# Eight seven-product units instead of seven per pair of column blocks in the first down projection, and an earlier last batch of activation sums

## The reference, cut to what matters

```python
def swiglu(x, w_gate, w_up, w_down):
    return (jax.nn.silu(x @ w_gate) * (x @ w_up)) @ w_down

h = h + 0.5 * swiglu(rms_norm(h, ffn1_norm), ffn1_w_gate, ffn1_w_up, ffn1_w_down)
...
h = h + 0.5 * swiglu(rms_norm(h, ffn2_norm), ffn2_w_gate, ffn2_w_up, ffn2_w_down)
```

## Time and profile before

| | us |
|---|---|
| median of 3 runs | 1835.87 (1835.83 to 1838.89) |
| the profiled execution | 1837.03 |
| its span, first to last instruction | 1834.9 |
| TensorE busy in the span | 1817.6 (99%) |
| VectorE busy | 1504.9 (82%) |
| ScalarE busy | 997.4 (54%) |
| mean clock granted to TensorE | 0.999 of full |

### The profile page before, as it was taken

One profiled execution on the slowest core, in us unless ns is written; L12 is line 12 of the kernel. 1 busy time (PEld: TensorE's weight loads), 2 busy tenths in 40 slices (PEclk: granted clock), 3 DMA queues, 4 the chain that ended last, 5 costly groups with the idle time before them and its releaser, 6 DMA issues.

```text
span 1834.9 us, 29704 instructions
## 1 busy us (share of the span) xinstructions
PE 1817.6 (99%) x10674; PEld 1544.7 (84%) x10674; DVE 1504.9 (82%) x1754; ACT 997.4 (54%) x1181; POOL 11.1 (1%) x23
## 2 busy tenths in 40 slices
PE   8999999999999999999999999999999999999998
PEld 7888888888888888999998878888888888888886
DVE  5888888888998986688966866688888888899996
ACT  7455555555555655754535665545555555555554
POOL 1000000000000000000000000000000000000000
PEclk9999999999999999999999999999999999999999
DMA  7767776777766778565433558577767677676664
GB/s 239 230 212 222 231 221 206 227 218 233 241 199 210 220 227 266 176 185 143 139 111 108 175 171 264 178 229 234 230 220 233 216 226 225 218 237 199 208 216 149
DMA packets 207850, 380.35 MB, mean 207 GB/s; under 512 B 16016, under 2 KB 35728, under 8 KB 207504
## 3 DMA queue, kind: packets, MB, share of 16 engines
q1 hardware_dynamic: 206768, 377.08, 65.3%
q10 hardware_dynamic: 480, 1.97, 0.3%
q0 software_dynamic: 512, 0.06, 0.0%
HBM read 360.19 MB, written 18.87 MB: 207 GB/s over the span
## 4 chain that ended last, share of the span: by engine, by line
PE 92%; DVE 3%; DMA 2%; ACT 1%; issue 1%; SPq 0%; ACTq 0%; DVEq 0%
PE psA L427 30%; PE psB L427 28%; PE psB L1231 6%; PE psT L438 5%; PE psM L438 5%; PE psA L438 5%; PE psA L1231 4%; PE psB L438 2%; PE psM L427 1%; DVE wlo L410 1%; DMA raw<-in_w_in 1%; PE psA L1242 1%; PE psB L650 1%; DMA raw<-in_ffn_w_down 0%; DVE y L1455 0%
## 5 line engine op out<-in xcount | busy, mean ns | idle before, releaser
L401 ACT CAST whi<-raw 128x1024 fp32r<-128x1024 f32 (+1 forms) x648 | 676.6, 1049 | 693.6 <-DVE raw L1455 186.1
L410 DVE TENSOR_TENSOR wlo<-raw,whi 128x1024 fp32r<-128x1024 f32 (+1 forms) x648 | 771.8, 1214 | 205.2 <-ACT whi L401 192.4
L427 PE MATMUL psA<-whi,xh 128*128 128x512 f32 (+1 forms) x576 | 221.8, 385 | 0.5 <-DVE wlo L410 0.5
L427 PE MATMUL psA<-whi,xl 128*128 128x512 f32 (+1 forms) x576 | 221.2, 384 | 0.0
L427 PE MATMUL psA<-wlo,xh 128*128 128x512 f32 (+1 forms) x576 | 221.2, 384 | 0.0
L427 PE MATMUL psB<-whi,xh 128*128 128x512 f32 x544 | 211.7, 389 | 0.0
L427 PE MATMUL psB<-whi,xl 128*128 128x512 f32 x544 | 211.6, 389 | 0.0
L427 PE MATMUL psB<-wlo,xh 128*128 128x512 f32 x544 | 211.6, 389 | 0.0
L427 PEld LDWEIGHTS psA<-whi,xh 128*128 128x128 f32 x576 | 108.4, 188 | 22.0 <-DVE wlo L410 0.7
L427 PEld LDWEIGHTS psA<-whi,xl 128*128 128x128 f32 x576 | 108.4, 188 | 21.3
L427 PEld LDWEIGHTS psA<-wlo,xh 128*128 128x128 f32 x576 | 108.4, 188 | 21.1
(11 more groups left out here) (511 smaller groups left out, 3436.7 us busy)
## 6 DMA issues: line engine op xcount, KB each, us to landing
raw<-in_ffn_w_gate SPq DMA_DIRECT2D x176, 512.0 KB, 4.5
raw<-in_ffn_w_up SPq DMA_DIRECT2D x176, 512.0 KB, 4.6
raw<-in_ffn_w_down SPq DMA_DIRECT2D x176, 512.0 KB, 4.5
raw<-in_w_in SPq DMA_DIRECT2D x80, 512.0 KB, 3.7
raw<-in_w_out SPq DMA_DIRECT2D x32, 512.0 KB, 4.3
quads_dram<-stage SPq DMA_DIRECT2D x88, 128.0 KB, 4.3
stage<-quads_dram SPq DMA_DIRECT2D x22, 512.0 KB, 4.3
x<-in_x SPq DMA_DIRECT2D x4, 512.0 KB, 7.6
```

What stands on the lines that cost most here:

```text
L401: nc.scalar.copy(whi[:, slot, :, 0:ncol], raw[:, slot, :, 0:ncol]).then_inc(hi_ready, 1)
L410: nc.vector.tensor_tensor(wlo[:, slot, :, 0:ncol], raw[:, slot, :, 0:ncol], whi[:, slot, :, 0:ncol].bitcast(F32), ALU.subtract).then_inc(l ...
L427: mm = nc.tensor.matmul(ps[:, tb, 0:ncol], lhs[:, k0 + t, tok], rhs[:, slot, t, 0:ncol], start=(first and t == 0 and p == 0 and tb != open ...
```

## The change

It sets two constants. UNITS gives the first network eight units in both pairs; each pair's list has then 36 items, with 14 lead, 10 inner and 4 tail plain ones in the first pair, and 6, 10 and 12 in the second. `down_order` spreads the 10 inner ones over 7 gaps as 1, 1, 2, 1, 2, 1, 2. `begin` becomes 36. SUMS_AT moves the fourth batch of sums, in both networks, from items 26 to 29 to items 22 to 25; in the first network the batch grows from one unit's sums to two units'.

```diff
-UNITS = ((7, 7), (7, 8))
+UNITS = ((8, 8), (7, 8))
...
-SUMS_AT = (5, 7, 9, 26)
+SUMS_AT = (5, 7, 9, 22)
```

## The result

The changed kernel takes 1845.80 us (median of 6 runs, 1844.07 to 1846.13), the kernel before, run beside it and counted with its earlier runs, 1838.74 (6 runs, 1835.83 to 1840.04). The ratio is 1.0040, with a 95% interval of 1.0027 to 1.0053: 7.1 us slower by the medians. The profiled execution took 1844.07 with a span of 1842.2, against 1837.03 and 1834.9.

The account below looks back on a forecast made before the run. TensorE, 99% busy, bounds the kernel while VectorE's thin lead holds. Removed -1.36, first pair +3.0, second +3.3, old wait -0.4: +4.5, median 1840.4 us; own range 1837.5 to 1843.4, 8-in-10 range reaching down to 1836.7.

Parts of the forecast that it names:

- the short cycles: VectorE, sums to sums with one plain group between units: 7.73 us against TensorE's 7.47, so 0.26 of lead lost each.
- Removed: First down projection: two more units take away six matmuls of 0.2265 us each, -1.36 us, all that can be gained.
- Lead at unit 0: How long VectorE's first remainder is ready before TensorE starts unit 0: 1.87 us first pair, 2.47 second.
- The cycles that VectorE's work fills: First down projection, unit-to-unit cycles with batch parts or x_lo and the turning of x: 9.07, 12.68, 11.63 us.
- ScalarE's 1.02: VectorE's idle time behind ScalarE's share of the first pair's fourth batch, between units 4 and 5: 1.02 us.
- Rival 3: First down projection: every load takes 5.0 us in short cycles too, 1.1 more each; +10.4, 1846.3 us; 8%.
- Unit 1 behind the first xq_store: Second pair: unit 1's second group waits for its load, so the cycle is 8.53 us, not 7.73; lead 1.41.
- Unit 6 behind the second xq_store: Second pair: loads queue behind eight stores, so unit 6's sums come 10.27 us after unit 5's; lead -3.14.
- The second xq_load ... nothing: Second pair: it follows unit 7's loads, its reader comes some 10 us later, so it costs nothing.
- The second network: Only the batch moves, four items up; lead of 0.2 us left behind it, wait between 0 and 0.3.
- Rival 1: First pair: VectorE stays ahead through the fourth batch, so no waits there; -1.36, perhaps -0.4 more, 1834.1 us; 12%.
- rival 2: Second pair, unit 6: the load behind the stores isn't late, pair costs 0.6 + 0.2; +2.0, 1837.9 us; 20%.

Follow-up runs that it names:

- e12: The changed kernel run again, unchanged: 1845.68 us against 1838.04 for the kernel before, ratio 1.0040.
- e5: The changed kernel with ScalarE's part of the fourth batch one item later: 1845.15 us, ratio 1.0039 to the kernel before.
- e9: e7 without the first network's fourth batch of sums (units 6 and 7 reuse sums of 4 and 5): 1838.83 us, ratio 1.0005 to the kernel before.
- e7: The changed kernel with the moves of e5 and e6, and the second xq_load one item later: 1840.81 us, ratio 1.0020 to the kernel before.
- e6: The changed kernel with the second xq_store issued behind unit 6's loads: 1843.08 us, ratio 1.0034 to the kernel before.
- e3: The kernel before with only the fourth batch moved from 26 to 22 in both networks: 1837.97 us, ratio 1.0002.
- e4: The changed kernel, eight units in both pairs, with the fourth batch left at 26: 1850.72 us, ratio 1.0068 to the kernel before.
- e2: The kernel before with eight units in the second pair only, a full fourth batch staying at 26: 1841.56 us, ratio 1.0019.
- e8: Kernel before with eight units in the second pair, its tail 10 instead of 12, second xq_store and xq_load behind unit 6: 1845.38 us, ratio 1.0043.
- e10: e7 with the fourth batch at items 11 to 14, ahead of the units: 1841.10 us, ratio 1.0018 to the kernel before.
- e11: The kernel before with its second xq_store and xq_load behind the loads of units 5 and 6: 1837.53 us, ratio 1.0000.

## Why the prediction was right in kind and too small

The forecast was 1840.4, +4.5 or 0.25%, in a range up to 1843.4; it came to 1845.8, +7.1 or 0.40%. The sign and the place are as forecast, the size isn't. Of the 5.4 between the two times 2.9 is the median of before, 1835.87 in the three runs shown and 1838.74 in six; the other 2.5 is terms of the sum that were taken too small. The range's top lay 7.5 above the median of before that it was counted from, and the measured difference, 7.1, is within that; so what put the time outside is the base as much as the terms. In the sum the step that failed is the loads' part of the cycles: the short cycles at 7.73 each, from one row, and the second `xq_load` at nothing. The two pairs lost 8.7 where 6.3 was forecast, 2.4 more: the short cycles made 1.8 of that, `xq_load` 0.7, unit 1 of the second pair 0.2 and its smaller lead at unit 0 0.3, less 0.5 for unit 6 and 0.1 elsewhere. Step by step:

- **Removed**, -1.36: matmuls 10674 to 10668, and short cycles without a wait take TensorE 7.48, as counted.
- **Lead at unit 0**: 1.87 forecast, 1.90 in the profile; in the second pair 2.47 and 2.19. "TensorE's lateness moves both engines alike" doesn't hold there: in e12 this lead is 0.96.
- **The cycles that VectorE's work fills**: 9.07, 12.68 and 11.63 forecast; 9.08, 12.78 and 11.64 measured. ScalarE's 1.02, read from the third batch, came exactly. e5 shows that it is that, e9 that the batch is the larger part of the first pair's loss (2.4 of 3.0 in e7).
- **The short cycles**, the step that failed. "A load that needs under 3.85 isn't felt" was right, and "one such pair in the second network went from sums to sums in 7.74" was one row. The sums that wait for the load started 3.95 to 4.35 after the first split's end; the five short cycles of the profile away from the turning of x took 7.84, 8.13, 8.23, 8.21 and 8.03, where 7.73 stood in the sum: 0.1, 0.4 and 0.5 in the first pair, 0.5 and 0.3 in the second. Rival 3, which put all loads at 5.0, had 1.1 for each. What was measured is about a third of that.
- **The first pair**: 3.0 forecast, 4.1 measured. The short cycles are 1.0 of the 1.1 between them.
- **Unit 1 behind the first xq_store**: 8.53 forecast, 8.77 here, and 8.7 to 9.9 over the profiles in which unit 1 stands there. A place with a burst beside it needs a range, and I gave a point.
- **Unit 6 behind the second xq_store**: 10.27 forecast, 9.81 measured; e6 shows that the stores are the cause (7.84 without). Right, with 0.5 too much.
- **"The second xq_load ... nothing"**: wrong. I checked its reader, which is indeed in time, and not its neighbour: it is issued right behind unit 7's loads, and the cycle to unit 7 became 10.92 against 10.19 of TensorE. That is 0.7 where "unit 7 recovers" stood. With it one item later, in e7, the cycle is 9.72.
- **The second pair**: 3.3 forecast, 4.6 measured.
- **The second network**: a lead of 0.2 forecast behind the batch, 0.14 measured; TensorE lost 0.35 there where 0 to 0.3 was allowed, 0.3 in e12 and 0.6 in e3.
- **Moved to 22**: "left at 26 it would be worse" holds, by 6 (e4).

Rival 1 falls by the first cluster of waits, rival 2 by the second: the load at unit 6 was 1.99 late. The first waits came at unit 4, not at 1 or 2, which is what was said to mark the forecast against rival 3. By the marks the mechanism is the forecast's; by the size, +7.1 between +4.5 and +10.4, it lies nearly halfway to rival 3, which is where the range ended. Its lower end is not what its parts give: ScalarE's wait hidden (-1.2) and half of the late load (-1.3) make 1837.9 and not 1837.5; nothing hangs on it.

What stays open: why the short cycles' loads need under 3.85 in one execution and up to 4.6 (a cycle of 8.48 in the first pair of e9) or 4.9 (8.81 in the second pair of e2) in another. That the longer ones end in a wait for a load is shown; no run changed the traffic beside them alone, so what makes the load late is not.

## What to carry to other kernels

Where one engine is at 99% and a second at 91% in the stage that changes, write down how far ahead the second one is at each hand-over, and walk the new order through cycle by cycle: work-filled cycles come out within 0.1 us, and the sum of busy time says nothing. Give each cycle that ends in a load the spread of that load and not its best row, and for each transfer that moves, look at what it is issued next to, not only at who reads it. Trading TensorE work for VectorE work at 1.36 against 10.4 us pays only where that time is idle at that very place.

## What the runs showed of the hardware

**A load can be slow beside another transfer on its queue, also beside one issued after it.** A load of 512 KB took 4.6 us from issue to landing in the middle over this stage of the changed kernel, and 3.5 to 6.6. With `xq_load` (512 KB) right behind it, unit 7's second load took 5.8, 6.3 (e12), 6.1 (e6), 6.0 (e5), 6.2 (e2) and 5.9 (e8), in e4 alone 4.9; with `xq_load` one item later 4.6 (e7), 4.5 (e9) and 4.7 (e10). The cycle to unit 7 followed: 10.92, 11.42, 11.32, 11.15, 11.40 and 11.06, in e4 10.06; one item later 9.72, 9.72 and 9.89. With eight stores of 64 KB ahead of unit 6's loads the cycle there was 9.81, 9.10 (e12), 9.83 (e5), 9.47 (e2) and 11.18 (e4); with them right behind, 7.84 (e6), 7.87 (e7), 7.95 (e9) and 7.86 (e10). Stores right behind are not harmless everywhere: in e11 the load ahead of them took 5.8, in e6, e7, e9 and e10 3.8 to 3.9. No run tells why.

**The clock.** A long wait costs more than itself. In e4 TensorE stood still for 7.51; the window behind it, and the one after:
```profile
577.00:580.00 3.00, 3.00 (x8) 2.32 (x9) 2.93 (x5) 0.26 (x1) 0.00 (x0) 0.50 0.68 201
...
582.00:590.00 8.00, 8.00 (x37) 6.59 (x36) 4.26 (x4) 4.09 (x4) 0.00 (x0) 1.00 0.43 132
```
The granted clock is 0.50 there, 1.2 GHz, and the matmuls start 0.43 apart where they start 0.2265 apart at full clock, 2.4 GHz. From 576.73 to 581.31 eleven took 4.58 in place of 2.49: 2.1 us lost on top of the wait. It happens a second time in the same profile: TensorE waits 3.3 at unit 6 of the second pair, the granted clock from 677 to 680 us is 0.51, and seven matmuls take 3.05 in place of 1.59, 1.5 lost. Together these 3.6 cover the 1 to 3 by which e4's total lay above its expectation. In e8 the granted clock fell likewise, to 0.59 in the mean of the 5 us from 720, where the wait of 3.4 ends. In the changed kernel's stage no wait is longer than 2.4 and the clock stays at 1.00. The Trainium skill, TensorE: Matmul & The Clock Gate (Part 1: The HAM clock gate), has the clock at half rate after an idle stretch and at full rate again after a busy one; these traces agree.
